# The gate matrix of a product-key expert layer: the weighting of the left one-hot side moved to GpSimd in two of three units

## The reference, cut to what matters

```python
N_KEYS, PEER_HEADS, PEER_TOPK = 128, 8, 16
cand_i = top_i[..., 0, :, None] * N_KEYS + top_i[..., 1, None, :]
expert_idx = jnp.take_along_axis(cand_i, best_pos, axis=-1)   # 8 x 16 = 128 choices per token
gate = jax.nn.softmax(best_s, axis=-1)
u = jnp.take(expert_u, ic, axis=0)
act = jax.nn.gelu(jnp.einsum('cd,cjd->cj', xc, u), approximate=False) * gc
out = jnp.einsum('cj,cjd->cd', act, jnp.take(expert_v, ic, axis=0))
```

## Time and profile before

| | |
|---|---|
| median of three runs | 4627.26 us |
| the profiled execution, its own time | 4622.6 us |
| its span, first to last instruction | 4620.8 us |
| gate matrix, first one-hot operation to last copy of a bank | 2372.4 to 2500.2 us |
| granted TensorE clock, mean | 0.964 |
| TensorE busy share over the span | 92% |

### The profile page before, as it was taken

One profiled execution on the slowest core, in us unless ns is written; L12 is line 12 of the kernel. 1 busy time (PEld: TensorE's weight loads), 2 busy tenths in 40 slices (PEclk: granted clock), 3 DMA queues, 4 the chain that ended last, 5 costly groups with the idle time before them and its releaser, 6 DMA issues. The chain is left out here.

```text
span 4620.8 us, 61806 instructions
## 1 busy us (share of the span) xinstructions
PE 4239.9 (92%) x23132; PEld 3774.3 (82%) x23132; DVE 3205.6 (69%) x4943; ACT 1551.6 (34%) x2801; POOL 703.8 (15%) x627
## 2 busy tenths in 40 slices
PE   8999989979987989699977799999999999999994
PEld 6888855656767778587767799999999999999993
DVE  4444436746623644589457688898889999888997
ACT  2212213434431421222346333333333333333331
POOL 0000001123320000033620111111111111111110
PEclk9999989989999999799989899999999999999997
DMA  9999976775545549736537999999999999999995
GB/s 283 315 311 313 317 203 198 242 197 177 178 117 194 189 154 298 226 126 189 173 116 202 307 316 323 318 310 317 310 315 314 314 317 313 314 314 309 319 304 182
DMA packets 575824, 1182.07 MB, mean 256 GB/s; under 512 B 63432, under 2 KB 327472, under 8 KB 520784
## 3 DMA queue, kind: packets, MB, share of 16 engines
q1 hardware_dynamic: 505408, 809.55, 57.3%
q0 software_dynamic: 53120, 358.64, 21.5%
q10 hardware_dynamic: 17040, 10.49, 0.8%
HBM read 1009.07 MB, written 228.15 MB: 268 GB/s over the span
## 5 line engine op out<-in xcount | busy, mean ns | idle before, releaser
L102 PE MATMUL h_ps<-xs,h_ut 128*128 128x352 f32 x6144 | 1077.1, 324 | 36.4 <-DVE h_ut L96 36.4
L102 PE MATMUL h_ps<-h_a,h_v 128*128 128x352 f32 x6144 | 1081.2, 324 | 18.7 <-DVE h_a L96 10.9
L102 PEld LDWEIGHTS h_ps<-xs,h_ut 128*128 128x128 f32 x6144 | 1009.9, 188 | 36.9 <-DVE h_ut L96 36.9
L102 PEld LDWEIGHTS h_ps<-h_a,h_v 128*128 128x128 f32 x6144 | 1004.5, 189 | 28.3 <-DVE h_a L96 17.9
L102 PE MATMUL a_ps<-xt_hi,a_w 128*128 128x512 f32 x1792 | 553.1, 390 | 8.1 <-DVE a_w L96 8.1
L96 DVE TENSOR_TENSOR h_v<-h_v_raw,h_v 128x512 fp32r<-128x512 f32 x512 | 350.1, 684 | 73.6 <-ACT h_v L95 73.5
L102 PEld LDWEIGHTS a_ps<-xt_hi,a_w 128*128 128x128 f32 x1792 | 337.0, 188 | 78.5 <-issue 8.3
L95 ACT ACTIVATE h_v<-h_v_raw 128x512 fp32r<-128x512 f32 x512 | 318.2, 622 | 224.4 <-PE h_ps L102 224.3
L102 PE MATMUL a_ps<-xt_lo,a_w 128*128 128x512 f32 x896 | 349.1, 390 | 0.0
L2611 DVE SCALAR_TENSOR_TENSOR y_first<-h_rows,h_acts,y_first 128x2048 f32<-128x2048 f32 x128 | 300.1, 2345 | 0.0
L2605 DVE CUSTOM_DVE_ANT_0 h_rows<-h_rows,h_x_first 128x2048 f32<-128x2048 f32 x128 | 292.2, 2283 | 0.0
(11 more groups left out here) (355 smaller groups left out, 6663.7 us busy)
## 6 DMA issues: line engine op xcount, KB each, us to landing
h_v_raw<-in_peer_v SPq DMA_DIRECT2D x128, 1024.0 KB, 9.0
h_u_raw<-turned_d SPq DMA_DIRECT2D x144, 512.0 KB, 9.4
a_raw<-in_w_in SPq DMA_DIRECT2D x28, 2048.0 KB, 12.4
a_xin<-in_peer_u SPq DMA_DIRECT2D x224, 256.0 KB, 7.8
turned_d<-a_xin SPq DMA_DIRECT2D x56, 1024.0 KB, 6.8
raw_d<-in_peer_u SPq DMA_DIRECT2D x448, 128.0 KB, 4.2
h_u_raw<-raw_d SPq DMA_DIRECT2D x112, 512.0 KB, 8.7
yt_last<-sums_d SPq DMA_DIRECT2D x125, 176.0 KB, 4.5
```

The lines of the kernel that those rows point to most:

```text
L102: mm = pe.matmul(out, lhs[a], rhs[b], start=(first and n == 0), stop=(last and n == 2))
```

## The change

In the units whose right side VectorE makes (two of three, 59 of 88), the left side is now one comparison over 128 x 4 x 128 elements on VectorE, with the second keys broadcast, and with no weighting. It counts up `names_made`. GpSimd waits for that, multiplies the tile in place by the broadcast gates in one TENSOR_TENSOR over the same 128 x 512 elements, and counts up `weighted`, for which TensorE now waits too in these units. The right side stays as it was. The 29 units of ScalarE keep the four small operations for their left side.

```diff
@@ gate_matrix
+        names_made, weighted = sem("names_made"), sem("weighted")
+        def weighted_by(u):
+            return u // 3 * 2 + u % 3 + 1
+        def of_quad(n, v, c):
+            return by_choice[n][:, c, v * QUAD:(v + 1) * QUAD].unsqueeze(2).broadcast_to([P, QUAD, NKEY])
@@ gpsimd
+            for u in range(UNITS):
+                if not by_act(u):
+                    n, v = divmod(u + SKIP, NQ)
+                    pool.wait_ge(kept, n + 1)
+                    pool.wait_ge(names_made, weighted_by(u))
+                    pool.tensor_tensor(left[u % RING][:, :, :], left[u % RING][:, :, :], of_quad(n, v, 2), ALU.mult)\
+                        .then_inc(weighted, 1)
@@ tensor
                 if by_act(u):
                     pe.wait_ge(right_made, u // 3 + 1)
+                else:
+                    pe.wait_ge(weighted, weighted_by(u))
@@ vector
-                for i in range(QUAD):
-                    t = v * QUAD + i
-                    second, gate = (by_choice[n][:, c, t:t + 1] for c in (1, 2))
-                    ins = dve.tensor_scalar(left[u % RING][:, i, :], iota_f[:, :], second, gate, ALU.is_equal, ALU.mult)
-                if not by_act(u):
-                    wide = [P, QUAD, NKEY]
-                    ins = dve.tensor_tensor(
-                        right[u % RING][:, :, :], iota_f[:, :].unsqueeze(1).broadcast_to(wide),
-                        by_choice[n][:, 0, v * QUAD:(v + 1) * QUAD].unsqueeze(2).broadcast_to(wide), ALU.is_equal)
+                if by_act(u):
+                    for i in range(QUAD):
+                        t = v * QUAD + i
+                        second, gate = (by_choice[n][:, c, t:t + 1] for c in (1, 2))
+                        ins = dve.tensor_scalar(left[u % RING][:, i, :], iota_f[:, :], second, gate, ALU.is_equal,
+                                                ALU.mult)
+                else:
+                    names = iota_f[:, :].unsqueeze(1).broadcast_to([P, QUAD, NKEY])
+                    dve.tensor_tensor(left[u % RING][:, :, :], names, of_quad(n, v, 1), ALU.is_equal)\
+                       .then_inc(names_made, 1)
+                    ins = dve.tensor_tensor(right[u % RING][:, :, :], names, of_quad(n, v, 0), ALU.is_equal)
                 ins.then_inc(ones_made, 1)
```

## The result

The changed kernel has a median of 4646.3 us in five runs (4641.6 to 4653.6), the kernel before 4628.7 in five; the ratio is 1.0044, 95% interval 1.0033 to 1.0056. It is slower by some 20 us (17.6 by the medians). The forecast was 4661.6 us; the direction and the taking of turns came out, and the size was 34 where 18 to 20 were measured.

What follows compares the result with a forecast made beforehand. VectorE was taken to bound the gate-matrix stage; 29 periods, each 1.16 us longer, give 33.6 us, the last unit 0.7, together plus 34.3, so a median of 4661.6 us; range for 8 in 10: 4634 to 4680.

Steps and rivals of the forecast that it cites:

- VectorE bounds the stage; two wide comparisons for eight small operations save 0.84 us a period: Gate matrix: VectorE alone would need 3.44 us per three-unit period instead of 4.28.
- The engines take turns: Gate matrix: VectorE and GpSimd transfer strictly by turns; GpSimd's work, 2.24 us a period, lands on VectorE's queue.
- The first rival: Gate matrix: the engines don't block each other; period 3.44 us, 4603.7 us in all; chance 5%.
- the third: Rival, gate matrix: each engine holds the other off for its whole duration; period 6.56 us, 4694 us; chance 5%.
- The small operations are blocked too: Every third unit's four small VectorE operations wait for GpSimd; period 5.44 us, without this rule 4.54.
- the second rival: Gate matrix: small operations run under GpSimd's second multiplication; period 4.54 us, 4635.5 us in all; chance 14%.
- A GpSimd turn takes 1.12 us: Gate matrix: each 128x512 multiplication ends 1.12 us behind VectorE's release, two per period.
- a bound below it: GpSimd's multiplication from the one-input AFFINE_SELECT's 0.63 us: about 0.5 us, period 4.2, 4625 us; chance 3%.
- W0: GpSimd's in-place multiplication for the first unit of a period, forecast to wait for that unit's right side, then take 1.12 us.
- A1: VectorE's left comparison in a period's second unit, forecast to wait for GpSimd's first multiplication and end 0.55 us behind it.
- The signs that rest on it: In the changed trace: some comparisons 1.7 to 1.8 us, one small operation of four 1.2 to 1.4, multiplications 1.5 to 1.7.
- The tail, TensorE, the stores: Stage end: last unit plus 0.7 us, products and copy behind it unchanged; TensorE's slower clock fits the period; stores don't bind.

Runs made afterwards that it cites:

- the fill: Changed kernel with GpSimd's multiplication replaced by a fill of the same tile with ones, all waits kept: 4600.3 us, ratio 0.9948 to the kernel before.
- halving the dose: Against the changed kernel, the change made in one of three units only, the others keeping four small operations: 4634.1 us, ratio 1.0018 to the kernel before.
- the flat input: Changed kernel with GpSimd multiplying the left tile by itself, not by the broadcast gates: 4644.7 us, ratio 1.0046 to the kernel before.
- the one wait: Changed kernel with VectorE's wait for free buffers taken once for a pair of wide units: 4648.6 us, ratio 1.0050 to the kernel before.
- all units weighted: Changed kernel with GpSimd weighting the left side of all units, key numbers in SBUF: 4662.8 us, ratio 1.0076 to the kernel before.

## Why the prediction was right in direction and long in size

- *VectorE bounds the stage; two wide comparisons for eight small operations save 0.84 us a period.* Right: without the multiplication the period is 3.43 (3.44 worked out), and the stage 25 us shorter.
- *The engines take turns.* Right, and shown from four sides: taking away GpSimd's reading (the fill), its operation, or VectorE's second SBUF input, and halving the dose. The first rival, no blocking, is dead; so is the third, blocking for whole durations (6.56 us a period). On that the Trainium skill says the shared ports are held for the full instruction (SBUF — State Buffer, "SBUF: two separate sides"); the trace doesn't bear it out as a way to add up durations: behind a release a multiplication of 1.04 us ends after 0.90, and a small operation of 0.33 after 0.08.
- *The small operations are blocked too.* Right, by the run with the comparisons in PSUM (0.74 and 0.08 behind the release). This is what parts the forecast from the second rival.
- *A GpSimd turn takes 1.12 us.* This is the term that was mis-sized: 0.90 and 0.92. Two turns a period are 2.24 against 1.82, 0.42 of the 0.54 us by which the period was too long: 12 us of the 15 by which the sum of 34 exceeded the stage's 19.2. The row taken was of the same operation and size but with two flat inputs; the text named the broadcast input as unseen and put a bound below it, then chose the nearer-looking row.
- *W0 goes ahead of A1, and only the first small operation waits.* Wrong in order: from the second period on VectorE keeps its turn through all four comparisons, and the first multiplication lands behind the fourth, the second between the first two small ones. In time it matters less: two small operations hide their start in a wait (0.08 each) where one was forecast (small ones 0.68 in place of 0.85), against 0.05 more for A1. That is 0.12 a period, 3.5 us. That a wrong order did so little harm was luck; nothing in the working foresaw it. The signs that rest on it failed: A1 (1.7 to 1.8 us) was held up only once, at the start of the stage, as 1.53; two small operations waited (1.06 and 1.08) and not one; the multiplications were 2.56 and 1.04 and not 1.5 to 1.7. TensorE's idle time was to end on GpSimd's g_left; the profile puts most of it down to VectorE's right side, though the starts show the wait for GpSimd (2434.80, 0.10 behind it).
- *The tail, TensorE, the stores.* The last unit cost 0.5 and not 0.7, and TensorE's clock another 0.7 that was not in the sum. The granted clock was 1.00 (2.4 GHz) from 2380 to 2498 us before, and 0.86 on average after, so for a part of the time at the 1.2 GHz level, while TensorE waited and worked by turns; as forecast, the new period has room for it, but the last unit has not. The stores and the next stage were moved, not lengthened.

What stays open is who gets the next turn. Take every end of a comparison at which a multiplication was waiting and another comparison with both inputs in SBUF was next, in the changed kernel and in the runs with the flat input, the one wait, all units weighted, and the small operations from PSUM. Count VectorE's operations from the last one that had waited or followed idle time, that one included. With one or two GpSimd got in (112 of 112), with five or more VectorE kept its turn (178 of 180), and there was nothing between. Where a small operation from SBUF was next instead, GpSimd got in in all 116 cases. That the instruction issued first goes first, as forecast, is false: the multiplication at 2432.14 was issued ahead of the comparison at 2432.52. That it depends on how far VectorE's queue has run ahead would fit, also the seven idle periods of the run with one wait, but no run was made to test it.

## What to carry to other kernels

Before work is moved from VectorE to GpSimd, add up their turns: operations of VectorE with two SBUF inputs or at double rate, and operations of GpSimd that read, run one after the other, so an offload pays only where the work that VectorE is rid of takes longer than GpSimd's turn (here 0.43 us a unit against 0.90, of which 0.75 are left after what VectorE starts meanwhile). Look for a way round the turns before giving up the offload: one input of the comparison put into a free PSUM bank turned a loss of 19 us in the stage into a gain of 13, and with the small operations gone, of 28. And when a busy engine's mean duration for a form grows while its count doesn't, it is waiting inside its instructions; the idle columns don't show it.

## What was not expected of the hardware

- GpSimd's TENSOR_TENSOR over 128x512 lasts 1.04 us with a broadcast second input or one tile on both inputs, and 1.27 with two different flat tiles.
- A comparison with one input in PSUM lasts 0.67 us, as with both in SBUF (0.68). The f32 operation with two per-partition scalars over 128 elements lasts 0.40 from PSUM in place of 0.33, and follows the one in front at 0.32 in place of 0.26.
- VectorE may keep its turn ahead of a waiting GpSimd operation for three comparisons, 1.7 us (multiplications of 2.56 us).
